# A hybrid encoder layer: half of the input projection by Strassen's seven products ahead of all mixers, and the mixers placed on a timetable

## The reference, cut to what matters

```
h = rmsnorm(x)                       # (1024, 2048)
proj = h @ w_in                      # (2048, 7552): 59 tiles of 128 columns
A: 6 heads, HGRN2 recurrence: tiles f, q, i, gate      (24 tiles)
B: 5 heads, band attention:   tiles q, k, v, gate      (20 tiles)
C: 5 heads, retention:        tiles q|k, v, gate       (15 tiles)
y = concat(group outputs) * silu(gates)                # (1024, 2048)
out = rmsnorm(x + y @ w_out) * final_gain
```

## Time and profile before

| | us |
|---|---|
| median of 2 runs | 1910.11 (1909.78 to 1910.44) |
| the profiled execution | 1908.2 |
| its span, first to last instruction | 1906.4 |
| TensorE busy | 1857.8 |
| VectorE busy | 926.4 |
| GpSimd busy | 885.8 |
| ScalarE busy | 457.7 |

### The profile page before, as it was taken

How to read it: one execution, slowest core, us unless ns; L and a number is a source line. 1 busy time by engine, 2 the same in 40 slices (tenths; PEclk the granted TensorE clock), 3 DMA queues, 4 the chain that set the end, 5 groups by cost and what they waited for, 6 DMA issues and landing times.

```text
span 1906.4 us, 24920 instructions
## 1 busy us (share of the span) xinstructions
PE 1857.8 (97%) x9118; PEld 1543.6 (81%) x9118; DVE 926.4 (49%) x1223; ACT 457.7 (24%) x624; POOL 885.8 (46%) x811
## 2 busy tenths in 40 slices
PE   8899999999999999999999999999999998999996
PEld 6688888888888888888888888888888886888884
DVE  7855747475746611313131322332322346777987
ACT  7313222222213110202020201321211222333442
POOL 6545445454545444453544444444545550154451
PEclk9999999999999999999999999999999999999998
DMA  7111111111111111111111111211111239577875
GB/s 246 45 34 55 39 39 50 39 55 39 50 39 52 38 61 45 47 49 38 60 36 62 39 57 44 69 49 49 58 39 58 71 110 380 193 245 247 285 255 220
DMA packets 91947, 175.49 MB, mean 92 GB/s; under 512 B 10730, under 2 KB 11503, under 8 KB 91892
## 3 DMA queue, kind: packets, MB, share of 16 engines
q1 hardware_dynamic: 85690, 159.05, 25.0%
q10 hardware_dynamic: 6202, 15.69, 2.4%
HBM read 157.91 MB, written 16.79 MB: 92 GB/s over the span
## 4 chain that ended last, share of the span: by engine, by line
PE 82%; DVE 8%; DMA 3%; ACT 3%; issue 2%; SPq 1%; POOL 0%; ACTq 0%; DVEq 0%; POOLq 0%
PE prj L535 60%; PE prj L851 9%; PE mix L624 2%; DMA y_in<-y_scratch 2%; PE mix L696 2%; PE mix L679 2%; PE mix L580 1%; DVE arena L1578 1%; PE mix L689 1%; ACT arena L892 1%; DVE w_lo L1523 1%; SPq L444 1%; PE mix L619 1%; DMA arena<-in_xT 1%; ACT arena L895 1%
## 5 line engine op out<-in xcount | busy, mean ns | idle before, releaser
L535 PE MATMUL prj<-mv_hi,w_hi 128*128 128x512 f32 x1824 | 575.1, 396 | 0.3
L535 PE MATMUL prj<-mv_lo,w_hi 128*128 128x512 f32 x1824 | 564.0, 390 | 0.0
L535 PE MATMUL prj<-mv_hi,w_lo 128*128 128x512 f32 x1824 | 562.6, 390 | 0.0
L490 POOL TENSOR_TENSOR pool_pad<-eps_sb 128x1 f32<-128x1 f32 x236 | 68.5, 290 | 763.1 <-PE prj L535 742.9
L535 PEld LDWEIGHTS prj<-mv_hi,w_lo 128*128 128x128 f32 x1824 | 342.7, 188 | 73.1
L535 PEld LDWEIGHTS prj<-mv_lo,w_hi 128*128 128x128 f32 x1824 | 342.7, 188 | 72.8
L535 PEld LDWEIGHTS prj<-mv_hi,w_hi 128*128 128x128 f32 x1824 | 333.5, 188 | 64.8 <-issue 1.8
L491 POOL TENSOR_SCALAR w_hi<-w_raw 128x512 fp32r<-128x512 f32 x236 | 373.6, 1583 | 0.0
L494 POOL TENSOR_TENSOR w_lo<-w_raw,w_hi 128x512 fp32r<-128x512 f32 x236 | 318.3, 1349 | 19.7
L892 ACT ACTIVATE arena<-arena 128x1024 f32<-128x1024 f32 (+1 forms) x121 | 124.2, 1036 | 382.3 <-DVE arena L1245 167.8
L514 POOL TENSOR_TENSOR raws<-raws 128x512 f32<-128x512 f32 x80 | 111.3, 1393 | 181.4 <-DMA raws<-in_wo 181.4
(11 more groups left out here) (146 smaller groups left out, 1790.9 us busy)
## 6 DMA issues: line engine op xcount, KB each, us to landing
w_raw<-in_w SPq DMA_DIRECT2D x236, 256.0 KB, 2.5
raws<-in_wo SPq DMA_DIRECT2D x184, 256.0 KB, 3.7
y_in<-y_scratch SPq DMA_DIRECT2D x80, 256.0 KB, 4.6
arena<-in_xT SPq DMA_DIRECT2D x16, 512.0 KB, 5.0
y_scratch<-arena ACTq DMA_DIRECT2D x16, 512.0 KB
arena<-in_xT SPq DMA_DIRECT2D x32, 256.0 KB, 7.8
outT<-arena SPq DMA_DIRECT2D x32, 256.0 KB, 2.1
arena<-y_scratch ACTq DMA_DIRECT2D x15, 256.0 KB, 5.0
```

The lines of the kernel that those rows point to most:

```text
L490: nc.gpsimd.tensor_tensor(pool_pad[:], eps_sb[:], eps_sb[:], ALU.mult)
L535: last = nc.tensor.matmul(prj[pair][:, cols], wt[q][:, kk, :], mv[:, k, cols], start=(k == 0 and wt is w_hi and mv is mv_hi), stop=(k == K ...
```

## The change

1. The first 30 of 59 input tiles are computed as 15 pairs by Strassen's seven products (`IN_PRODUCTS`): 105 steps of 24 matmuls, in two granules of 12, with no mixer stage between them. The moving operands are sums of blocks of x (512 frames each): SP loads the two terms, ScalarE scales one, VectorE adds the other, ScalarE rounds and VectorE takes the remainder. The products are added into `acc_in`, which lies where `mv_hi` and `mv_lo` will be; finished quarters are multiplied by the inverse norm (`in_scale`) and stored to `z_dram`. The operands of product j+1 are made during product j. The x blocks for the standard tiles come in during the last product (`h_high`, `h_low`), the last three after it.
2. In these steps GpSimd adds the two raw weight blocks (5 of the 7 products) straight into the ring (`w_sum` lies on `w_lo`), ScalarE rounds and VectorE takes the remainder. There are 6 raw buffers.
3. The other 29 tiles are computed as before, with a stage after every 12 matmuls, 232 places in all (called slots below). ScalarE moves 26 of them unscaled to `stage`, SP stores them to `z_dram`. The last three go straight to the last unit of C.
4. All other mixer inputs are loaded from `z_dram` by ScalarE's queue. For tiles from 30 on, VectorE multiplies what has landed by `rstd` in place of the eviction (`landed`).
5. The mixers' stages stand at fixed slots. The program orders of ScalarE and VectorE within a unit stay as they were, with loads and evictions (`evict_until`) put between. The loops over units are unrolled. L490 is gone.
6. The output projection is as before but for the order of a few loads.

```diff
+IN_PAIRS = 15
+IN_TILES = 2 * IN_PAIRS
+IN_STEPS = 7 * IN_PAIRS
+IN_RAWS = 6
+STD = TO - IN_TILES
+DIRECT = TO - 3
+A_EACH, B_EACH, C_EACH = 20, 12, 9
+B_FROM, C_FROM, C_LAST = 127, 187, 2 * NG * (STD - 1)
...
+            pe.wait_ge(ones_ready, 3)
+            for n in range(2 * OPEN):
+                in_product(n, range(GRAN * (n // OPEN), GRAN * (n // OPEN) + GRAN))
+            for st in range(OPEN, IN_STEPS):
+                pe.wait_ge(in_acc_done, st - 3)
+                for q in range(2):
+                    in_product(2 * st + q, range(GRAN * q, GRAN * q + GRAN))
...
+            for u in range(A_HEADS):
+                b = A_EACH * u
+                put(b + 6, a_diag(u, 0))
+                put(b + 8, a_diag_level(u))
+                put(b + 9, a_level(u, 1))
+                put(b + 11, a_level(u, 2))
+                put(b + 12, a_level(u, 3))
+                put(b + 13, a_level(u, 4))
+                put(b + 15, a_level(u, 5))
+                put(b + 16, a_near(u))
+                put(b + 17, a_kdtr(u))
+                put(b + 18, a_state(u))
+                put(b + 20, a_out(u))
+                put(b + 24, a_ss(u, 0))
+                put(b + 25, a_ss(u, 1))
+            for i in range(B_HEADS):
+                b = B_FROM + B_EACH * i
+                put(b, b_vtr(i))
+                for n in range(BLK + 2):
+                    put(b + 1 + n, b_visit(i, n))
+            for i in range(C_HEADS - 1):
+                b = C_FROM + C_EACH * i - (i == C_HEADS - 2)
+                put(b + 2, c_vtr_k(i))
+                put(b + 3, c_scores(i))
+                put(b + 4, c_state(i))
+                put(b + 6, c_out(i))
+                put(b + 8, c_ss(i, 0))
+                put(b + 9, c_ss(i, 1))
+            put(C_LAST + 1, c_vtr_k(C_HEADS - 1))
+            put(C_LAST + 3, c_scores(C_HEADS - 1))
+            put(C_LAST + 5, c_state(C_HEADS - 1))
...
             def a_mix(u):
+                b = A_EACH * u
                 sigmoid(2 * u)
+                evict_until(b + 5)
...
             def a_mix(u, before=nothing):
-                g = 4 * u
-                silu_evict(g + 1, 1, 2 * u)
+                if u > 0:
+                    dve.wait_ge(parts_split, A_PARTS * u)
+                silu_load(2 * u)
                 lv_diff_of(u, 0)
                 before()
                 silu_finish(2 * u, Q, A_DK ** -0.5)
...
+            def landed(t, dst, arrived, count):
+                dve.wait_ge(arrived, 16 * count)
+                if t < IN_TILES:
+                    return nc.vector.memset(land_pad[:, t - TB:t - TB + 1], 0.0)
+                return tt(arr(dst), arr(dst), rstd[:], ALU.mult)
...
+            def load_x(k):
+                if k < 2:
+                    sp.wait_ge(in_comb_lo, HK + IN_COMBS)
+                else:
+                    sp.wait_ge(h_lo, k - 1)
+                sp.dma_start(x_entry[k % 2][:], xT[k]).then_inc(xe_in[k % 2], 16)
```

More of the change, by code:

```diff
@@ new lines, in in_comb_at, with entry_count @@
+        def in_comb_at(v):
+            j, p = divmod(v, IN_PAIRS)
+            return [HK * j + p - OPEN] if j < 6 and OPEN <= p < OPEN + HK else []
+        entry_loads = [[len(in_terms(idx)) for idx in range(e, IN_COMBS, 2)] + [1] * HK for e in range(2)]
+        def entry_count(e, use):
+            return 16 * sum(entry_loads[e][0:use + 1])
+        IN_SQUARES = HK * 4
+        sum_done = {0: HK + 2 * HK - 1, 1: HK + 3 * HK - 1}
+        spills = []
+        for v in range(IN_STEPS):
+            j, p = divmod(v, IN_PAIRS)
+            if j == 4:
+                spills.append((v, p, C21))
+            if j == 5:
+                spills.append((v, p, C12))
+                if p > 0:
+                    spills.append((v, p - 1, C22))
+            if j == 6:
+                if p == 0:
+                    spills.append((v, IN_PAIRS - 1, C22))
+                spills.append((v, p, C11))
@@ L380, in _ @@
         def _(sp):
[L381 to L396, removed]
@@ new lines, in _, with put, stage @@
+            stages = [nothing] * (2 * NG * STD)
+            def put(slot, *parts):
+                before = stages[slot]
+                def stage():
+                    before()
+                    for part in parts:
+                        part()
+                stages[slot] = stage
+            for u in range(A_HEADS):
[13 more added lines that the diff above has]
+                put(b + 25, a_ss(u, 1))
@@ L1097, in _ @@
                                      scale=0.0).then_inc(c_zeroed, 1)
-            with act.Fori(0, C_HEADS - 1) as i:
+            for i in range(C_HEADS - 1):
                 c_unit(i)
@@ L1401, in _ @@
             a_mix(0)
-            with dve.Fori(1, A_HEADS) as u:
+            for u in range(1, A_HEADS):
                 a_decay(u)
@@ L1457, in _ @@
             b_unit(0, first=True)
-            with dve.Fori(1, B_HEADS) as i:
+            for i in range(1, B_HEADS):
                 b_unit(i)
@@ L1511, in _ @@
             dve.wait_ge(ctab_in, 32)
-            with dve.Fori(0, C_HEADS // 2) as j:
-                c_unit(2 * j, 0)
-                c_unit(2 * j + 1, 1)
-            c_unit(C_HEADS - 1, 0, last=True)
+            for i in range(C_HEADS - 1):
+                c_unit(i)
+            c_unit(C_HEADS - 1, last=True)
             dve.wait_ge(y_ready, UNITS)
```

849 lines of the change are left out of this document (598 added, 251 removed).

## The result

The changed kernel takes 2019.36 us (median of 2 runs, 2017.81 to 2020.91) against 1910.11 before: 1.0572 times as long, 95% interval 1.0526 to 1.0617. The forecast was 2038 with 1970 to 2095. The profiled execution took 2020.91 us, with a span of 2019.1.

A forecast was written before the change was run, and what follows sets the result against it. TensorE, busy 1857.8 of 1906.4 us, was taken as the bound. 1906.4 - 81.7 - 24.2 (old start) + 19 + 1 (norm products) + 6 + 209.9 (waits, clock) = 2036.4; with 1.8 around it 2038 us, range 1970 to 2095.

The forecast's parts named there:

- Seven products: Input projection's first 30 tiles: 360 fewer matmuls at 0.227 us each, -81.7 us.
- Their feed: Loads and operands for the seven products: +6 us (0 to 45), for products 6 and 7.
- Start: Kernel's start: old losses of 24.2 us go, new ones of 19 us (14 to 27) come; net -5.
- A to A: Boundaries between mixer A's units: a 15.3 us chain gets 3.2 us of slots; TensorE waits 12.1 us, five times.
- short chains: Rival: less contention and clock loss, 10.5 us per A boundary, 145 us of waits in all, 1973 us; chance 0.15.
- First unit: Mixer A's first unit: its diagonal sum is ready after its slot, a wait of 15.6 us (11 to 20).
- B: Mixer B: waits of 12.5 us inside units, 5.9 four times between units, 5.3 each into B and into C.
- C: Mixer C's boundaries: waits of 10.5 us twice, 13.3, and 7.8 for the last unit; 42.1 together.
- Clock: Half-speed clock around waits: 2.8 us for each of 16 waits of 5 us or more, 45 us (30 to 60).
- Entry to the output projection: Output projection keeps its losses; two late weight loads there may cost 0 to 3 us.
- the timetable holds: Rival: chains hide behind the slots, about 1830 us; break-even at 80 us of waits; chance 0.05.
- Weights come too late: Rival: loads land in 7 to 8 us near full DMA share; products 6 and 7 lose 45 us, 2077; chance 0.15.

The follow-up runs named there:

- run 3: Kernel after with the seventh product's x loads one step later in SP's queue; 2011.87 us against 2019.4.
- Run 2: Kernel after with unused products filling TensorE's waits ahead of mixer A's diagonal sums (40 per unit, 56 for the first); 2011.55 us against 2019.4.
- run 4: Kernel after with mixer B's next bias fetched earlier and the next unit's V scaled within the unit before; 1990.3 us against 2019.4.
- run 5: Kernel after with mixer A's next query SiLU computed within the norm of the unit before; 1981.29 us against 2019.4.
- run 6: Kernel after with mixer C's next rotation within the norm of the unit before, and tiles 56 and 57 reported right behind their evictions; 2001.67 us against 2019.4.
- run 7: Kernel after with the edits of run 3, run 4, run 5 and run 6 together; 1936.2 us against 2019.4.
- run 8: run 7 plus V scaled before mixer C's table product and mixer B's first bias, and 60 unused products in mixer A's first wait; 1897.78 us, 0.9923 of the kernel before.

## Why the prediction was right

The mechanism is the one forecast: the timetable gives a unit's boundary one slot or two where VectorE's and ScalarE's chains, whose order is unchanged, need 12 to 18 us, and TensorE stops with everything behind it. The forecast was 18.6 us too long, and the total came out closer than its parts: two terms were too large by 33 us together, and 16 us that it did not have partly made up for it, which is luck. By its own steps:

- **Seven products, -81.7.** Until product 7 they run at the pace taken: 300 us (from 100 to 400) without a gap, and the 50 us in which product 6 moves the most cost 0.75 (the last fence below). The forecast's ceiling of 387 GB/s was not in the way. Loads landed in 3.8 us (median), near the 4.1 taken.
- **Their feed, +6.** The place was wrong. Product 6, where I saw the peak, lost under 1 us (0.75 idle in the fullest 50). Product 7 lost about 10 us, for a reason I had not priced: each x load waits on SP's queue for VectorE's split of an earlier block, and the next weights stand behind it (run 3). Another 5.3 us went at the first standard tile: 15 in all. By this the stage ended at 603.4 where I said about 600.
- **Start, +19.** Between 0 and 100 us TensorE is busy 84.2 us at a mean clock of 0.97: 15.8 of waits and near 3 of clock, 19 in all (20 by the 351 matmuls that the trace has there).
- **A to A, 12.1 each.** 10.1 to 10.4. The chain's parts were right. Its last step, 5.8 us by the rows of before, took 4.2, with GpSimd no longer beside it. This was the rival of short chains, taken at 10.5 for this boundary, and here it held.
- **First unit, 15.6.** 14.6.
- **B.** Between units 5.9 forecast, 4.1 to 5.0 found; into B 5.3 forecast, 5.2 found; into C 3.4 for 5.3; inside B, 12.5 forecast and 6.9 found by the waits of L890 and L897 (3.2 and 3.7).
- **C.** 10.5, 10.5, 13.3 and 7.8 forecast, 42.1 in all. Found 7.9, 9.9, 10.7 and 11.4 (two waits at the transposes for each of the first three), 39.9 in all. The fourth is the size that I got from the wrong place: it stands ahead of tile 58, whose bank VectorE had emptied at 1631.7 and reported at 1639.9, behind the whole rotation:

```profile
1630.52 1.22 DVE L1516 TENSOR_TENSOR arena<-prj,rstd 128x1024 f32<-128x1024 f32 x1
...
1639.86 0.06 DVE L1963 MEMSET land_pad<- 128x1 f32 x1
```

- **Clock, 2.8 for each of 16 waits.** Run 2 found 2.1 for each of six (2.0 to 2.6, by the kernel that it is set beside), run 4 about 2 for each of four. There are 18 waits over 3.8 us outside the start, so about 38 instead of 45.
- **Entry to the output projection, 0 to 3.** 4.7, 3.9 and 1.2 us of waits, against 5.7 before at its step. Its matmuls then span 322 us (1677.2 to 1999.3), and 324 before (1562.5 to 1886.7).

The waits of the timetable are 164.9 in the forecast and, summed by the numbers above, 51.0 + 14.6 + 6.9 + 17.6 + 5.2 + 3.4 + 39.9 = 138.6. These 26 us are the term that was mis-sized (10.5 of them at A's boundaries and the first unit, 6 inside B, 6 between B's units, 2 each into C and in C), with 7 for the clock; 9 more on the feed went the other way. The measured terms give 1906.4 - 81.7 - 24.2 + 19 + 1 + 15 + 138.6 + 38 = 2012, 7 short of the span, which the entry to the output projection covers in part and nothing else was measured for.

Of the rivals, "the timetable holds" falls with 138.6 us of waits, 177 with the clock, where 80 would have been even. Runs 4 to 8 show what its condition was: with the chains reordered the same slots do hold to 3.4 us, save the first unit's, which run 8 fills and does not shorten, and the kernel with the seven products then gains 0.8% over the kernel before. "Short chains" had 145 us of waits and clock and the forecast 209.9. The 177 found lie halfway between the two, so the choice between them was a matter of size and not of mechanism. "Weights come too late" falls in its condition, slow landing near the ceiling: product 6 ran at the highest rate almost without loss, and run 3 sped product 7 up at a higher rate. Weights did come late in product 7, by the order of the queue, and that cost about 10 us and not 45.

What stays open: which half of run 4's edit did the work, what the 60 unused products of run 8 are worth alone, and whether the 8.1 us in the output projection, whose chain shows a load of 10 us from issue to landing, can be moved by an earlier issue. None was tried. Nor was the seven products' part run without the packed timetable; its 81.7 us rest on the count of matmuls and their pace.

## What to carry to other kernels

When work is packed closer on the engine that bounds a kernel, an engine's average load says little: here the others showed 62% and less, and TensorE waited 138.6 us for them. Take each hand-over between units as a chain, add the durations in program order on the other engines, and set it against the slots left for it. Where such a wait shows up, look first for an operation that is queued behind another's wait without needing it (here V behind the bias or the decay table, the report of an emptied bank behind a rotation, weights behind an x load). Moving it took no added work in runs 3 to 6, but part of a wait can come back elsewhere: 7.6 us in run 5, 4.2 and 7.0 in run 6. Durations on VectorE read while GpSimd was busy (1.67 and 2.34 us here) can be too long for a kernel in which it starves (1.22).

## What was not expected of the hardware

- The granted clock's mean over a stage overstates its cost. In mixer A's stage it was 0.94, but filling the waits gave back 2.1 us per unit of 85, 2.5% (up to 2.6 us, 3%), since the clock falls late in a wait (at about 811 for a stop at 805.9) and half of the slow time is idle.
- One core moved 362 GB/s at a DMA share of 1.00 for 50 us, and TensorE lost 0.75 us in them. The window of the kernel after:

```profile
450.00:500.00 50.00, 49.25 (x217) 40.23 (x216) 42.83 (x57) 18.62 (x33) 25.43 (x19) 1.00 1.00 362
```
